# A spare buffer of 32 bytes in front of the row vector of the conditioning input

## The chip, the cores and the metric

The kernel runs on one core of one Trainium2 chip. The metric is the time of one execution on the device, in microseconds (us), lower is better. On the core five engines work side by side: TensorE (PE in the profile, its weight loads are listed apart as PEld), VectorE (DVE), ScalarE (ACT), GpSimd (POOL) and SyncE (SP), which issues most of the DMAs. Each has an instruction stream of its own, and semaphores order them. SBUF is the on-chip memory of 128 partitions, in which a buffer takes the same byte range in every partition. PSUM has eight banks that take TensorE's results.

## What is computed

Two transformer-like blocks, one after the other, on one sequence of 512 tokens of width 1024, all in float32. The first is a gated short convolution beside a stick-breaking attention, then an MLP, with scales and shifts made from a conditioning vector `c`. The second is a gated convolution of 31 taps beside a rotary attention with grouped keys, then attention to a memory of 256 rows, then a gated feed-forward layer with a convolution of 3 taps. Cut to what matters:

```python
def first_block(x, c, ...):
    mod = c @ w_ada[l] + b_ada[l]
    sh1, sc1, gt1, sh2, sc2, gt2 = jnp.split(mod, N_MOD, axis=-1)
    h = modulate(rms_norm(x, g_pre_mix[l]), sh1, sc1)
    proj = h @ w_in[l]
    ...
    x = x + gt1[:, None, :] * rms_norm(mix_out, g_post_mix[l])
    h2 = modulate(rms_norm(x, g_pre_mlp[l]), sh2, sc2)
    ff = jnp.square(jax.nn.relu(h2 @ w_mlp_in[l])) @ w_mlp_out[l]
    x = x + gt2[:, None, :] * rms_norm(ff, g_post_mlp[l])

def second_block(x, mem, ...):
    x = x + rmsnorm(parallel_mixer(rmsnorm(x, ...), ...), norm_mix_post[l])
    x = x + rmsnorm(memory_cross_attention(rmsnorm(x, ...), rmsnorm(mem, ...), ...), norm_mem_post[l])
    x = x + rmsnorm(conv_gated_ffn(rmsnorm(x, ...), ...), norm_ffn_post[l])
```

## The kernel before

Every large product runs on TensorE as three products of rounded parts. A weight slab of 1 MB (128 partitions by 2048 numbers) comes from HBM into one of the two halves of `w_raw`. GpSimd makes `w_hi` of it (the number rounded to the float32r format, line 602) and `w_lo` (the rest, line 604). ScalarE and VectorE make the same two parts of the other operand (`ht_hi` and `ht_lo`, `hq_hi` and `hq_lo`, `yt_hi` and `yt_lo`, `hf_hi` and `hf_lo`). `mm3`, lines 687 to 689, then issues hi by hi, lo by hi and hi by lo into one PSUM bank. In the profile the name in front of the comma is the moving operand, which streams past the array, and the one behind it is the stationary operand, which is loaded before each matmul: `bank<-ht_hi,w_hi` moves 512 tokens of `ht_hi` past 128 columns of `w_hi`, and `bank<-w_hi,hq_hi` moves 512 columns of `w_hi` past 128 tokens of `hq_hi`.

The stages follow one another: the first 33 us load `x` and the modulation weights (`ada_w`, seven buffers of 4 KB a partition) and sum them on VectorE (`ada_acc`, line 1662), then come the input product of the first block, its attention (about 209 to 340 us), the output product, the MLP (430 to 770 us), the second block's mixer with the convolution of 31 taps (`av`, shared by VectorE, GpSimd and TensorE, about 855 to 985 us), the attention to the memory, and the feed-forward layer (1200 to 1565 us).

All of SBUF is laid out by `sb(...)` calls, in program order, lines 265 to 375: a buffer starts where the last one ended, rounded up to a multiple of 32 bytes, and buffers in a closed `lend` or `ph` stack give their place to the next ones. Nothing else in the program depends on where a buffer lies. What matters below is the start of each buffer modulo 64 bytes, by the layout of the built program:

| Buffers | start modulo 64, before |
|---|---|
| `w_raw`, `w_hi`, `w_lo`, `x`, `ident`, `ones`, `vec` (all made ahead of `c_row`) | 0 |
| `c_row`, `gpost`, `stat`, `smx`, `qks`, `eps_t` | 0 |
| `xn`, `tmp`, `p2b`, `p2c`, `p2d`, `ht_hi`, `ht_lo`, `ada_w`, `ada_acc`, `mem`, `mem_k`, `mem_v`, `m1`, `at1`, `q1`, `k1`, `mg`, `yt_hi`, `yt_lo`, `sgb`, `hq_hi`, `hq_lo`, `hr`, `facc`, `qm`, `pm`, `ptm`, `av`, `uc`, `hf_hi`, `hf_lo`, `facc2` | 32 |
| `b1`, `ay`, `p2a`, `pt2`, `tap_m`, `rope`, `rope_m`, `qf` | 0 |

Of the kernel before, what the change touches and what calls it, by code (L numbers as in the profile page):

```python
# [25 lines left out]
P = 128  # L26
# [228 lines left out]
def build(nc, A, out):  # L255
    with ExitStack() as ctx:
        def sb(name, shape, dt=F32, where=None):
            return (where or ctx).enter_context(nc.sbuf_tensor(name, shape, dt))
# [15 lines left out]
        mod = sb("mod", [P, 4, DC])  # L274
        cvec = sb("cvec", [P, DC])
        mod_g = sb("mod_g", [P, DC])
        c_row = sb("c_row", [DC, P])
        gpost = sb("gpost", [P, 2, D])
        stat = sb("stat", [P, 64])
# [1899 lines left out]
```

How the kernel before makes its waits and increments, by code:

```python
    def after(self):  # L161
        if self.last is not None:
            self.eng.wait_ge(*self.last)
# [257 lines left out]
            def wait_free(self, eng):  # L422
                if not self.first:
                    eng.wait_ge(psum_free[self.b], self.use)
# [1 line left out]
            def wait_full(self, eng):  # L426
                eng.wait_ge(psum_full[self.b], self.use + 1)
# [1 line left out]
            def wait_taken(self, eng):  # L429
                eng.wait_ge(psum_free[self.b], self.use + 1)
# [22 lines left out]
        @block.sync  # L453
# [6 lines left out]
            def load(view, src, at=None):  # L460
                nonlocal n
                num = n if at is None else at
                if at is not None or n >= 2:
                    sp.wait_ge(slab_split, num - 1)
                sp.dma_start(view[n % 2], src).then_inc(slab_loaded[n % 2], 16)
                n += 1
# [7 lines left out]
            def ada(i):  # L475
                r = i % ADA_BUFS
                if i >= ADA_BUFS:
                    sp.wait_ge(ada_used, i - ADA_BUFS + 1)
                s = i // DC
                sp.dma_start(ada_w[:, r], wada[:, i % DC, s * D:(s + 1) * D]).then_inc(ada_loaded[r], 16)
# [5 lines left out]
            win = w_rows(A["w_in"])  # L486
            i = 2 * DC
            for c0 in (512, 1024, 0, 1536, 2048, 2560):
                for s in range(2):
                    if n == 1:
                        sp.wait_ge(ada_used, 2 * DC)
                    load(raw4, win[:, 4 * s:4 * s + 4, c0:c0 + 512])
                    for _ in range(4 if n > 2 else 0):
```

## Time and profile before

| | us |
|---|---|
| median of 3 runs | 1587.15 |
| lowest and highest of them | 1586.88, 1588.55 |
| the profiled execution's own time | 1588.48 |
| its span, from the first to the last instruction | 1586.6 |
| PE busy in the span | 1512.0 (95%) |
| POOL busy | 864.2 (54%) |
| DVE busy | 735.4 (46%) |
| ACT busy | 413.6 (26%) |
| mean granted clock of TensorE | 0.984 |

The table is read from the top: the execution's own time is 1.9 us over its span, and 1.33 us over the median of the three timed runs. TensorE is busy in 95% of the span, and the others in about half of it or less. A busy TensorE says nothing of how fast each matmul went by, since matmuls overlap; for that the distance from one start to the next is read from the timeline.

### The profile page before, as it was taken

The page shows a single profiled execution, that of the slowest core. Times are in us where ns is not written, and L with a number is a line of the kernel's source. Part 1 is how long each engine was busy: PE and PEld are TensorE (multiplying, and loading weights), DVE is VectorE, ACT ScalarE, POOL GpSimd, SP SyncE. Part 2 cuts the span into 40 slices and gives each one's busy share as a digit, 9 for nine tenths or more (in the row PEclk, how much of TensorE's full clock was granted, in tenths as well). Part 3 has the DMA queues.
Part 4 walks back from the last instruction along what each step waited for, and adds up shares of the span by engine and source line. Part 5 has one row for each costly group of instructions (what it writes and reads, how often), then busy time and mean ns, then how long its engine had stood idle before and what let it go on. Part 6 is the DMA issues. An engine that isn't in the chain of part 4 may idle for free.

```text
span 1586.6 us, 18794 instructions
## 1 busy us (share of the span) xinstructions
PE 1512.0 (95%) x7119; PEld 1197.7 (75%) x7119; DVE 735.4 (46%) x1067; ACT 413.6 (26%) x833; POOL 864.2 (54%) x333
## 2 busy tenths in 40 slices
PE   3999999999999999999899899999998999999997
PEld 3788767778988888888798644688687788888886
DVE  6795167752831111112333976341516544455445
ACT  3101133331520100101334166452414211111113
POOL 1666344345665655556567994175054656565652
PEclk8999999999999999999999999999999999999999
DMA  8874221223323232322243101032021332323231
GB/s 323 333 267 156 94 80 54 82 80 104 120 80 106 80 106 81 104 88 97 85 135 99 61 1 53 27 107 94 27 80 54 106 106 80 106 79 106 80 106 53
DMA packets 91765, 161.87 MB, mean 102 GB/s; under 512 B 3453, under 2 KB 44337, under 8 KB 91697
## 3 DMA queue, kind: packets, MB, share of 16 engines
q1 hardware_dynamic: 88720, 155.20, 28.8%
q10 hardware_dynamic: 2977, 5.73, 1.0%
q8 instruction: 47, 0.77, 0.2%
q14 instruction: 21, 0.17, 0.0%
HBM read 158.82 MB, written 2.10 MB: 101 GB/s over the span
## 4 chain that ended last, share of the span: by engine, by line
PE 78%; DVE 13%; ACT 4%; POOL 2%; issue 2%; DMA 1%; POOLq 0%; SPq 0%; DVEq 0%; ACTq 0%
PE bank L687 24%; PE bank L689 24%; PE bank L688 24%; DVE bank L1662 3%; DVE bank L1658 1%; POOL w_lo L604 1%; DVE smx L2024 1%; PE bank L1090 1%; DVE ada_acc L1662 1%; DVE x L1658 1%; DVE ht_lo L1658 1%; DMA ada_w<-in_w_ada 1%; DVE q L1658 1%; PE bank L1161 1%; PE bank L1142 1%
## 5 line engine op out<-in xcount | busy, mean ns | idle before, releaser
L602 POOL TENSOR_SCALAR w_hi<-w_raw 128x2048 fp32r<-128x2048 f32 x119 | 229.5, 1928 | 630.4 <-PE bank L687 602.5
L604 POOL TENSOR_TENSOR w_lo<-w_raw,w_hi 128x2048 fp32r<-128x2048 f32 x119 | 554.4, 4658 | 9.9
L687 PE MATMUL bank<-ht_hi,w_hi 128*128 128x512 f32 (+1 forms) x1200 | 448.5, 374 | 13.7 <-DVE ht_lo L1658 8.2
L688 PE MATMUL bank<-ht_hi,w_lo 128*128 128x512 f32 (+1 forms) x1200 | 445.3, 371 | 0.0
L689 PE MATMUL bank<-ht_lo,w_hi 128*128 128x512 f32 (+1 forms) x1200 | 445.3, 371 | 0.0
L687 PEld LDWEIGHTS bank<-ht_hi,w_hi 128*128 128x128 f32 x1200 | 226.1, 188 | 62.4 <-DVE ht_lo L1658 10.3
L689 PEld LDWEIGHTS bank<-ht_lo,w_hi 128*128 128x128 f32 x1200 | 226.0, 188 | 43.4
L688 PEld LDWEIGHTS bank<-ht_hi,w_lo 128*128 128x128 f32 x1200 | 226.1, 188 | 42.5
L1662 DVE SCALAR_TENSOR_TENSOR uc<-bank,par,uc 128x511 f32<-128x511 f32 x88 | 66.0, 750 | 162.9 <-ACT uc L1628 161.2
L1658 DVE TENSOR_TENSOR facc<-bank,facc 128x512 f32<-128x512 f32 x104 | 72.0, 692 | 123.5 <-PE bank L689 115.8
L1628 ACT ACTIVATE uc<-bank,par 128x512 f32<-128x512 f32 x44 | 34.3, 780 | 268.6 <-PE bank L689 257.3
L687 PE MATMUL bank<-w_hi,hq_hi 128*128 128x512 f32 x256 | 101.3, 396 | 0.0
L688 PE MATMUL bank<-w_hi,hq_lo 128*128 128x512 f32 x256 | 101.3, 396 | 0.0
L689 PE MATMUL bank<-w_lo,hq_hi 128*128 128x512 f32 x256 | 101.3, 396 | 0.0
L1447 ACT ACTIVATE hr<-bank 128x512 f32<-128x512 f32 x32 | 19.2, 600 | 271.3 <-PE bank L689 270.5
L687 PE MATMUL bank<-w_hi,ht_hi 128*128 128x512 f32 x224 | 89.5, 399 | 0.0
L689 PE MATMUL bank<-w_lo,ht_hi 128*128 128x512 f32 x224 | 88.6, 395 | 0.0
L688 PE MATMUL bank<-w_hi,ht_lo 128*128 128x512 f32 x224 | 88.6, 395 | 0.0
L1662 DVE SCALAR_TENSOR_TENSOR ada_acc<-ada_w,cvec,ada_acc 128x1024 f32<-128x1024 f32 x42 | 74.8, 1781 | 17.8 <-DMA ada_w<-in_w_ada 14.3
L1658 DVE TENSOR_TENSOR bank<-bank,hr 128x512 f32<-128x512 f32 x32 | 22.4, 699 | 128.0 <-ACT hr L1447 128.0
L689 PE MATMUL bank<-w_lo,hf_hi 128*128 128x512 f32 x176 | 70.1, 398 | 0.0
L687 PE MATMUL bank<-w_hi,hf_hi 128*128 128x512 f32 x176 | 69.3, 394 | 0.1
(258 smaller groups left out, 2054.7 us busy)
## 6 DMA issues: line engine op xcount, KB each, us to landing
w_raw<-in_w_in SPq DMA_DIRECT2D x27, 1024.0 KB, 5.2
ada_w<-in_w_ada SPq DMA_DIRECT2D x48, 512.0 KB, 7.5
w_raw<-in_w_up SPq DMA_DIRECT2D x22, 1024.0 KB, 5.1
w_raw<-in_w_mlp_in SPq DMA_DIRECT2D x16, 1024.0 KB, 5.2
w_raw<-in_w_mlp_out SPq DMA_DIRECT2D x16, 1024.0 KB, 5.1
w_raw<-in_w_down SPq DMA_DIRECT2D x11, 1024.0 KB, 4.9
w_raw<-in_w_out SPq DMA_DIRECT2D x8, 1024.0 KB, 5.0
w_raw<-in_w_mem_kv SPq DMA_DIRECT2D x8, 1024.0 KB, 5.5
```

The source lines that it names most:

```text
L602: g.tensor_scalar(w_hi[:, r], w_raw[:, r], 1.0, 1.0, ALU.mult, ALU.mult).then_inc(slab_hi, 1)
L604: g.tensor_tensor(w_lo[:, r], w_raw[:, r], w_hi[:, r].bitcast(F32), ALU.subtract).then_inc(slab_split, 1)
L687: inc_free(pe.matmul(o, ah, bh, start=start, stop=False))
L688: pe.matmul(o, al, bh, start=False, stop=False)
L689: return pe.matmul(o, ah, bl, start=False, stop=stop)
L1090: ins = pe.matmul(t.ap[HD * j:HD * j + HD, :], v2[:, kc, v], pt2[:, j, kc], start=kc == 0, stop=kc == NT - 1)
L1142: ins = pe.matmul(t.ap[:, 0:NM], qm[:, 2 * h + c, qt * P:qt * P + P], mem_k[:, 2 * h + c, :], start=c == 0, stop=c == 1)
L1161: ins = pe.matmul(t.ap[:], mem_v[:, kc, h * MHD + c * P:h * MHD + c * P + P], ptm[:, kc], start=kc == 0, stop=kc == MT - 1)
L1447: st.done(act.activation(hr[:, m % 2], t.ap[:], ACT.Relu), hr_ready)
L1628: st.done(act.activation(uc[:, c], t.ap[:], ACT.Identity, scale=par[:, p, 2 + g, k:k + 1], bias=par[:, p, 6 + g, k:k + 1]), uc_ready)
L1658: do(v.tensor_tensor(o, a, b, op), sem, tile)
L1662: do(v.scalar_tensor_tensor(out=o, in0=a, scalar=s, in1=b, op0=op0, op1=op1), sem, tile)
```

## The change

One buffer of 8 numbers a partition (32 bytes) is made ahead of `c_row`. No instruction reads or writes it. All buffers made behind it, `c_row` among them, lie 32 bytes higher; `w_raw`, `w_hi`, `w_lo`, `x`, `ident`, `ones`, `before`, `not_before`, `vec`, `mod`, `cvec` and `mod_g` stay. The highest buffer still ends inside SBUF. Every engine has the same instructions in the same order with the same semaphores, only the addresses of operands differ, and line numbers behind the new line are one higher.

```diff
--- before.py
+++ after.py
@@ -274,6 +274,7 @@
         mod = sb("mod", [P, 4, DC])
         cvec = sb("cvec", [P, DC])
         mod_g = sb("mod_g", [P, DC])
+        spare = sb("spare", [P, 8])
         c_row = sb("c_row", [DC, P])
         gpost = sb("gpost", [P, 2, D])
         stat = sb("stat", [P, 64])
```

In the table of the section on the kernel, the second row of buffers goes from 0 to 32 modulo 64, the third from 32 to 0, the fourth from 0 to 32; the first stays at 0. Modulo 256, `ada_w` goes from 160 to 192, `gpost` from 0 to 32, and `mem` and `ada_b` from 224 to 0; `w_raw` stays at 128.

## Rows read from the trace of the kernel before

**Rows 1.** Page, head, busy time (share of span) by engine, instructions
```profile
span 1586.6 us, 18794 instructions
...
PE 1512.0 (95%) x7119; PEld 1197.7 (75%) x7119; DVE 735.4 (46%) x1067; ACT 413.6 (26%) x833; POOL 864.2 (54%) x333
```

**Rows 2.** Page, chain of work that ended last, shares of the span by engine
```profile
PE 78%; DVE 13%; ACT 4%; POOL 2%; issue 2%; DMA 1%; POOLq 0%; SPq 0%; DVEq 0%; ACTq 0%
```

**Rows 3.** Waits, whole span: who waited for whom, us in total, times, longest
```profile
POOL w_hi L602 <- PE bank L687: 602.5, 102, 38.9
```

**Rows 4.** Timeline, PE, `ht` moving past `w`: start us, us, engine, line, instruction
```profile
59.73 0.39 PE L687 MATMUL bank<-ht_hi,w_hi 128*128 128x512 f32 x1
...
61.83 0.40 PE L687 MATMUL bank<-ht_hi,w_hi 128*128 128x512 f32 x1
```

**Rows 5.** Timeline, PE, `w` moving past `hq`
```profile
479.62 0.40 PE L689 MATMUL bank<-w_lo,hq_hi 128*128 128x512 f32 x1
...
481.72 0.40 PE L689 MATMUL bank<-w_lo,hq_hi 128*128 128x512 f32 x1
```

**Rows 6.** Timeline, PE, 256 columns, where the clock rises from 1.2 to 2.4 GHz
```profile
1201.08 0.41 PE L689 MATMUL bank<-ht_lo,w_hi 128*128 128x256 f32 x1
...
1203.63 0.41 PE L689 MATMUL bank<-ht_lo,w_hi 128*128 128x256 f32 x1
...
1204.75 0.28 PE L689 MATMUL bank<-ht_lo,w_hi 128*128 128x256 f32 x1
...
1205.93 0.28 PE L687 MATMUL bank<-ht_hi,w_hi 128*128 128x256 f32 x1
```

**Rows 7.** Groups of PE by form: count, busy us, mean ns, idle before
```profile
L687 PE MATMUL bank<-ht_hi,w_hi 128*128 128x512 f32 x944 | 375.1, 397 | 6.7 <-POOL w_lo L604 5.5 <-DVE ht_lo L1658 1.2
...
L687 PE MATMUL bank<-w_hi,hq_hi 128*128 128x512 f32 x256 | 101.3, 396 | 0.0
...
L687 PE MATMUL bank<-w_hi,ht_hi 128*128 128x512 f32 x224 | 89.5, 399 | 0.0
...
L687 PE MATMUL bank<-w_hi,hf_hi 128*128 128x512 f32 x176 | 69.3, 394 | 0.1
L687 PE MATMUL bank<-yt_hi,w_hi 128*128 128x512 f32 x64 | 26.4, 413 | 1.7 <-DVE yt_lo L1658 1.7
...
L1078 PE MATMUL bank<-ident,p2c 128*128 128x128 f32 x32 | 5.0, 278 | 0.0
L1078 PE MATMUL bank<-ident,p2a 128*128 128x128 f32 x32 | 4.9, 276 | 0.0
```

**Rows 8.** Instructions on `av`: ns min/median/max, first and last start
```profile
L1662 DVE SCALAR_TENSOR_TENSOR bank<-av,vec,bank x58: 754/756/758, 863.1 to 975.2; 128x512 f32<-128x512 f32 x58
...
L1103 PE MATMUL bank<-av,tap_m x52: 590/592/697, 925.4 to 984.0; 128*128 128x512 f32 x52
L639 POOL TENSOR_SCALAR tmp<-av,vec x30: 682/692/1130, 858.5 to 944.8; 128x512 f32<-128x512 f32 x30
```

**Rows 9.** Groups of DVE by form, sums and parts of 512 numbers
```profile
L1658 DVE TENSOR_TENSOR facc<-bank,facc 128x512 f32<-128x512 f32 x104 | 72.0, 692 | 123.5 <-PE bank L689 115.8 <-DVE x L1662 0.5
...
L1658 DVE TENSOR_TENSOR x<-bank,x 128x512 f32<-128x512 f32 x32 | 22.1, 692 | 1.1
```

**Rows 10.** Timeline, GpSimd and VectorE at the start of the first attention
```profile
212.26 4.62 POOL L604 TENSOR_TENSOR w_lo<-w_raw,w_hi 128x2048 fp32r<-128x2048 f32 x1
...
213.60 3.43 DVE L1658 TENSOR_TENSOR m<-m,not_before 128x128 f32<-128x128 f32 x1
```

**Rows 11.** Instructions on `m`: ns min/median/max, first and last start
```profile
L1658 DVE TENSOR_TENSOR m<-m,not_before x32: 292/295/3435, 211.2 to 322.9; 128x128 f32<-128x128 f32 x32
```

**Rows 12.** Busy time by stretch, us, then clock, DMA share, GB/s
```profile
20.00:27.00 7.00, 4.33 (x24) 4.24 (x24) 6.47 (x6) 0.70 (x1) 0.00 (x0) 0.99 1.03 411
...
36.00:38.00 2.00, 2.00 (x11) 1.98 (x11) 1.57 (x6) 1.48 (x3) 2.00 (x2) 0.50 1.05 404
```

**Rows 13.** Instructions on `gpost`, time of its five loads to landing
```profile
DMA to landing us min/median/max: 3.7/4.8/12.0
```

## The prediction, on record before the changed kernel ran

> **What bounds the kernel now.** I read the head of the page first: TensorE is busy for 1512.0 of 1586.6 us, the next engine, GpSimd, for 864.2 [rows 1], and the mean granted clock is 0.984 (table above). The chain of the work that ended last says the same: 78% of it is TensorE [rows 2], and GpSimd, which prepares the weights, waited for TensorE 102 times, 602.5 us in all [rows 3]. So nearly anywhere the time is the number of matmuls times the distance from one start to the next. The groups by form give the number: the hi by hi matmuls of 512 columns are 944 + 256 + 224 + 176 + 64 = 1664, and lines 688 and 689 have as many each, 4992 in all [rows 7]. The distance comes from the timeline, not from the durations in the groups, which overlap: nine starts take 61.83 - 59.73 = 2.10 us, 233.3 ns each [rows 4].
>
> That distance is not what the array itself would need, and this is what makes a change of addresses worth a look. Where the clock was still at 1.2 GHz, matmuls of 256 columns started 2.55 us / 12 = 212.5 ns apart; at 2.4 GHz ten of them took 1.18 us, 118 ns each [rows 6]. Half of 212.5 is 106, so at full clock some 12 ns for 256 columns, or by the same share 233.3 - 212.5 = 21 ns for 512 columns, come from something that does not speed up with the clock. If that something is the reading of SBUF, the start of an operand could bear on it.
>
> **The change, part by part.** It adds a buffer that nothing reads or writes, and no instruction, DMA or wait is added, removed or moved. What is left is the cost of an address that is 32 bytes higher, for each kind of reader and writer.
>
> Matmul, moving operand. Before, `ht` starts at 32 modulo 64 and `w` at 0. With `ht` moving the distance is 233.3 ns [rows 4]; with `w` moving nine starts take 481.72 - 479.62 = 2.10 us, 233.3 ns again [rows 5]. The two roles are exchanged between these stretches, so each of the two starts has been seen as the moving and as the stationary operand, at one price to within 0.01 us over nine matmuls, or 1.1 ns each. The mean durations of the five groups, 394 to 399 ns without the small one of `yt` (413), say the same [rows 7]. Moving `ht`, `yt` and stationary `hq`, `hf` from 32 to 0 is therefore 4992 x 0 = 0 us. The bound from the resolution is 4992 x 1.1 = 5.5 us either way; I take 0, because the same 233 ns recurs over the whole program.
>
> Matmul, plain float32. The convolution of 31 taps reads `av` from tap k on, that is from 31 starts 4 bytes apart, which pass both 0 and 32 modulo 64. Of 52 matmuls the median is 592 ns and the shortest 590; a few reach 697, too few to move the median, and a price of half the starts would move it [rows 8]. Transposes of `p2c` (32 modulo 64) and `p2a` (0) take 278 and 276 ns on average [rows 7]. Cost 0.
>
> VectorE and GpSimd. The same sliding reads take 754 to 758 ns on VectorE, all 58 of them, and a median of 692 ns on GpSimd [rows 8]. A sum into `x` (0 modulo 64) and one into `facc` (32) both take 692 ns [rows 9]. If the 4 ns of the first spread were all the address, some 1000 VectorE instructions would cost 4 us at most, of which 13% lie on the chain [rows 2]: 0.5 us. I take 0. GpSimd's two large steps work on `w_raw`, `w_hi` and `w_lo` alone, which do not move.
>
> DMA. `w_raw` stays, so only the opening, where VectorE waits for `ada_w`, could feel it. While the loads go to `ada_w` (32 modulo 64) the queues move 411 GB/s, and while they go to `w_raw` (0 modulo 64) 404 GB/s, both with the engines fully busy [rows 12]. If `ada_w` at 0 took the other rate, the 33 us ahead of the first product would change by 33 x 7 / 411 = 0.6 us; I take 0 and keep 0.6 both ways. `gpost` goes from 0 to 32; its loads take 3.7 to 12.0 us to land [rows 13], two of them under the first product and one in each later stage, long before their use, and would have to become several times longer to be seen.
>
> The sum is 0 against the profiled execution's own 1588.48 us, which lies 1.33 us above the median of the three runs. Against the median the forecast is 1587.15, say 1587.2 us.
>
> [...]
>
> **The rivals.** (a) *A pair of starts that has not been seen, and is cheaper.* In every float32r matmul before, one operand is at 0 and the other at 32 modulo 64; after, both are at 0. The exchange of roles above excludes a price of either alone, not of the pair. If the 21 ns over the half-clock distance are a collision between the read of the moving operand and the load of the next stationary one, and equal starts end it, the kernel gains up to 4992 x 21 = 105 us and lands at about 1482. For it speaks only that the 21 ns are unexplained. Against it: the surplus grows with the moving columns (12 ns at 256, 21 at 512) while the stationary load is the same 128 columns [rows 4, 6], so it does not look like a collision with the load. 4%.
>
> [...]
>
> (b) *The same pair, and dearer; slower.* Place: the same 4992 matmuls. If equal starts make the two reads meet where they now pass each other, by as much as the surplus that is already there, the cost is the same 105 us with the other sign, 1692 us. It decides early: 3.2 us / 4992 = 0.64 ns a matmul is already 0.2% of the time. The transposes are a small counter-example: `p2a` and `ident` both start at 0 and are no slower than `p2c` with `ident` [rows 7], but they read at half the rate. 3%.
>
> (c) *Other meetings of GpSimd and VectorE.* At 213.60 us a VectorE multiply took 3.43 us and ended 0.15 us after GpSimd's 4.62 us subtraction [rows 10], where the median of its kind is 0.295 us [rows 11]: it waited for it, by 3.1 us, in the attention stage, where VectorE is on the chain. A shift of a few tenths of a microsecond could add or take away such a meeting. But the streams have no new length that would shift them, and the three runs of before, in which DMA timing differs anyway, agree within 1.7 us. One meeting gives 1584 or 1590; to pass 0.2% it takes more than one. 3% on each side.
>
> (d) *The change does nothing because the layout hides it*, for instance if buffers were rounded to 64 bytes. They are rounded to 32, so all later buffers do move; if not, the time would be 1587 too.
>
> **How the numbers follow.** No effect: 87%, 1587.2, with its own spread from the runs of before (1586.9 to 1588.6), the 0.6 us of the opening and one meeting of (c), 3.1 us, each way: 1584.0 to 1590.3. That range leaves out (a), (b) and the far part of (c), less than 2 in 10, so it stands as the range. About 0.2% (3.2 us) is what a measurement of this kernel can tell from no change. Faster by more: 4% of (a) and 3% of (c), 7%. Slower by more: 3% of (b) and 3% of (c), 6%. Within 0.2%: the rest, 87%.
>
> **What would show it right or wrong.** In the changed kernel's profile the starts of nine matmuls near 60 and near 480 us should again take 2.10 us; the groups of `ht`, `hq` and `hf` should keep 394 to 399 ns; VectorE's taps 756 ns, sums into `facc` 692 ns; the stretch of 20 to 27 us about 411 GB/s. If the nine starts take less than 2.09 or more than 2.11 us, (a) or (b) is true and the step "each start has been seen, so the pair is free" has failed. If the distances are the same and the time is not, the difference must stand in the waits: in the durations of `m` on VectorE between 209 and 325 us (c), or in the start of the first product at 39 us (DMA).

## The result, and the profile after

The changed kernel took 1578.17 us, the median of six runs from 1573.54 to 1583.45, against 1588.27 us for the kernel before in its six runs (1586.88 to 1588.55). The ratio is 0.9938, with a 95% interval of 0.9915 to 0.9961: it is 0.6% faster, by 10.1 us, and its runs differ by 9.9 us where those of before differ by 1.7. The forecast of no change was wrong, and the time lies below the range of 1584.0 to 1590.3.

The page of the changed kernel, head, busy time by engine and the chain's shares (beside [rows 1, 2]):

```profile
span 1575.5 us, 18794 instructions
...
PE 1500.7 (95%) x7119; PEld 1200.9 (76%) x7119; DVE 731.9 (46%) x1067; ACT 413.4 (26%) x833; POOL 868.7 (55%) x333
...
PE 82%; DVE 10%; ACT 3%; POOL 2%; issue 1%; DMA 1%; POOLq 0%; SPq 0%; DVEq 0%; ACTq 0%
```

TensorE's busy time fell by 11.3 us with the same 7119 matmuls, and the span by 11.1. The busy times of the other engines moved by at most 4.5 us. The place is found on the timeline of PE, in three kinds of stretch; each pair of lines is nine matmul starts apart. `ht` moving past `w`, as in [rows 4]:

```profile
59.99 0.39 PE L688 MATMUL bank<-ht_hi,w_hi 128*128 128x512 f32 x1
...
62.05 0.39 PE L688 MATMUL bank<-ht_hi,w_hi 128*128 128x512 f32 x1
```

`w` moving past `hq`, as in [rows 5]:

```profile
480.03 0.39 PE L690 MATMUL bank<-w_lo,hq_hi 128*128 128x512 f32 x1
...
482.13 0.40 PE L690 MATMUL bank<-w_lo,hq_hi 128*128 128x512 f32 x1
```

`w` moving past `hf`, in the last stage, after the change and then before it:

```profile
1252.11 0.39 PE L690 MATMUL bank<-w_lo,hf_hi 128*128 128x512 f32 x1
...
1254.17 0.39 PE L690 MATMUL bank<-w_lo,hf_hi 128*128 128x512 f32 x1
```

```profile
1255.07 0.40 PE L689 MATMUL bank<-w_lo,hf_hi 128*128 128x512 f32 x1
...
1257.17 0.40 PE L689 MATMUL bank<-w_lo,hf_hi 128*128 128x512 f32 x1
```

With `ht` moving the nine starts take 2.06 us, 228.9 ns each, where they took 2.10 us. With `w` moving past `hq` they still take 2.10 us. With `w` moving past `hf` they take 2.06 where they took 2.10. So three stretches that looked alike before (233.3 ns all) now part. The mean durations of the groups by form hide most of this; the lines beside [rows 7]:

```profile
L688 PE MATMUL bank<-ht_hi,w_hi 128*128 128x512 f32 x944 | 372.0, 394 | 6.1 <-POOL w_lo L605 5.3 <-DVE ht_lo L1659 0.8
...
L688 PE MATMUL bank<-w_hi,hq_hi 128*128 128x512 f32 x256 | 101.3, 396 | 0.0
```

The mean of the `ht` group went from 397 to 394 ns while the distance went down by 4.3. The other readers of shifted buffers are where they were. Instructions on `av` and on `m` (beside [rows 8, 11]):

```profile
L1663 DVE SCALAR_TENSOR_TENSOR bank<-av,vec,bank x58: 754/756/756, 857.2 to 970.4; 128x512 f32<-128x512 f32 x58
...
L1104 PE MATMUL bank<-av,tap_m x52: 590/592/697, 920.6 to 979.2; 128*128 128x512 f32 x52
L640 POOL TENSOR_SCALAR tmp<-av,vec x30: 688/692/1147, 852.5 to 938.3; 128x512 f32<-128x512 f32 x30
```

```profile
L1659 DVE TENSOR_TENSOR m<-m,not_before x32: 292/294/3447, 209.7 to 320.3; 128x128 f32<-128x128 f32 x32
```

Sums into `facc` still take 692 ns, and the loads of the opening (the stretch of 20 to 27 us, all into `ada_w`, as in [rows 12]) moved 408 GB/s for 411.

**Where the 11.1 us of span come from.** Over all steps in the two traces, 2832 matmuls with `ht` moving came 4.3 ns closer each (233.3 to 229.0), which is 12.2 us; 528 with `w` moving past `hf` came 4.2 ns closer, which is 2.2 us. The matmuls of 256 columns, whose distances I worked out from the starts in the two traces, went two ways: 960 with `ht` or `mt` moving from 116.8 to 117.8 ns (1.0 us lost), 192 with `w` moving past `mt` from 118.2 to 113.5 (0.9 us gained). Together 14.3 us. Some 3 us were given back, most of them in two places: the first product began at 39.5 us for 39.0, and in the second attention the granted clock stayed at 0.50 for longer. Busy time by stretch, before and then after; the column behind those of the engines is the granted clock:

```profile
905.00:916.00 11.00, 5.50 (x26) 3.77 (x26) 7.53 (x7) 2.66 (x4) 10.09 (x11) 0.77 0.00 0
```

```profile
905.00:916.00 11.00, 8.48 (x15) 3.50 (x16) 3.02 (x5) 2.58 (x5) 10.09 (x11) 0.53 0.00 0
```

The mean granted clock of these 11 us is 0.77 before and 0.53 after; ahead of the fall TensorE had waits between short pieces of work in both kernels (busy for 2.59 us of 905 to 911 before and for 0.83 us of 900 to 905 after). The low stretch went from 911.0 to 917.8 us before (6.8 us) and from 905.6 to 915.9 us after (10.2 us). The part of the stage that took 105.1 us before (901.7 to 1006.7) took 106.7 us after (895.1 to 1001.9).

### The profile page after: what moved, and what is told of

Same layout as the page of the kernel before. It is cut to its first block, busy times and chain, and to the rows that moved or that the text cites. A ratio compares the mean times of both kernels' runs of the same rounds, so it can differ in the third digit from the quotient of the medians.

```text
span 1575.5 us, 18794 instructions
## 1 busy us (share of the span) xinstructions
PE 1500.7 (95%) x7119; PEld 1200.9 (76%) x7119; DVE 731.9 (46%) x1067; ACT 413.4 (26%) x833; POOL 868.7 (55%) x333
## 4 chain that ended last, share of the span: by engine, by line
PE 82%; DVE 10%; ACT 3%; POOL 2%; issue 1%; DMA 1%; POOLq 0%; SPq 0%; DVEq 0%; ACTq 0%
PE bank L688 25%; PE bank L690 25%; PE bank L689 25%; DVE bank L1663 2%; DVE bank L1659 1%; POOL w_lo L605 1%; DVE smx L2025 1%; PE bank L1091 1%; DVE ada_acc L1663 1%; DVE x L1659 1%; DMA ada_w<-in_w_ada 1%; DVE ht_lo L1659 1%; PE bank L1162 1%; PE bank L1143 1%; DVE m L1659 1%
## 5 line engine op out<-in xcount | busy, mean ns | idle before, releaser
L603 POOL TENSOR_SCALAR w_hi<-w_raw 128x2048 fp32r<-128x2048 f32 x119 | 232.8, 1956 | 612.6 <-PE bank L688 585.5
L688 PEld LDWEIGHTS bank<-ht_hi,w_hi 128*128 128x128 f32 x1200 | 226.4, 189 | 56.6 <-DVE ht_lo L1659 10.1
L689 PEld LDWEIGHTS bank<-ht_hi,w_lo 128*128 128x128 f32 x1200 | 226.4, 189 | 39.5 <-issue 0.2
L689 PE MATMUL bank<-w_hi,hf_lo 128*128 128x512 f32 x176 | 69.3, 394 | 0.0
```

The lines of the kernel that those rows point to most:

```text
L603: g.tensor_scalar(w_hi[:, r], w_raw[:, r], 1.0, 1.0, ALU.mult, ALU.mult).then_inc(slab_hi, 1)
L688: inc_free(pe.matmul(o, ah, bh, start=start, stop=False))
L689: pe.matmul(o, al, bh, start=False, stop=False)
```

## The experiments

### The changed kernel once more

The kernel is the changed one, unedited.

> The changed kernel once more, for a second profile and for the spread of its times, which went from 1573.5 to 1583.5 us in six runs where the kernel before stayed within 1.7 us. If the distance between matmul starts is fixed by addresses alone, this profile shows the same distances as the first one of the changed kernel (228.9 ns with ht moving, 229.1 with w moving past hf, 233.3 with w moving past hq or ht), and the spread comes from elsewhere. If the distance depends on a phase that differs between executions, some of these groups differ from the first profile by 1 ns or more, and explain a difference in time of 3 us or more.

1577.78 us (1574.88 to 1578.68, four runs), ratio 0.994, interval 0.9923 to 0.9957: the gain is there again. The distances with 512 columns were 228.96 ns with `ht` moving and 233.32 with `w` moving past `hq`, to 0.01 ns as in the first profile. The 256-column matmuls were not: of the first two groups with `mt` moving, 117.8 and 117.8 ns in the first profile, one had 113.3; the last long group with `ht` moving had 113.3 for 117.8. `yt` in its first product had 232.4 for 233.6. These account for about 1 of the 2.6 us by which the two spans (1575.5 and 1572.9) differ. The other 1.6 us arose between 178 and 186 us, where the granted clock was 0.50 for 6.8 us in the first profile and for 3.4 us in the second. Busy time by stretch, in the first profile and then in the second:

```profile
178.00:189.00 11.00, 11.00 (x39) 7.96 (x39) 5.51 (x12) 0.59 (x1) 3.99 (x2) 0.69 0.13 50
```

```profile
178.00:189.00 11.00, 11.00 (x46) 7.89 (x46) 5.29 (x12) 0.74 (x2) 5.25 (x2) 0.84 0.13 50
```

In the same 11 us TensorE got 39 matmuls in at a mean granted clock of 0.69, and 46 at 0.84. So the starts of the buffers fix most distances, at some of them more than one pattern is possible (117.8 or 113.3 ns), and the length of the low stretches of the clock (6.8 or 3.4 us) moves the time as well.

### 64 bytes instead of 32, and everything 32 bytes higher

```diff
-        spare = sb("spare", [P, 8])
+        spare = sb("spare", [P, 16])
         c_row = sb("c_row", [DC, P])
```

> The spare buffer is 64 bytes instead of 32: ht, hq, hf and the others lie 64 bytes higher than before and start at 32 modulo 64 again. Theory A (the start modulo 64 bytes decides): 233.3 ns everywhere, about 1588 us. Theory B (any change of the distance between the two operands decides, with a period over 64 bytes): distances other than 233.3 ns in at least one group, and a time that differs from 1588 by more than 3 us.

```diff
+        spare = sb("spare", [P, 8])
         w_raw = sb("w_raw", [P, 2, SLAB])
...
-        spare = sb("spare", [P, 8])
         c_row = sb("c_row", [DC, P])
```

> The spare buffer of 32 bytes stands in front of w_raw instead of c_row, so that every buffer lies 32 bytes higher, w_hi and w_lo too: ht is where it is in the changed kernel, and its distance to w is that of before. Theory C (the place of the two operands relative to each other decides): 233.3 ns everywhere, about 1588 us. Theory D (the start of ht, hf alone decides): 228.9 ns with ht moving, about 1578 us, as the changed kernel.

Both diffs are against the changed kernel. With 64 bytes the time was 1592.2 us, ratio to the kernel before 1.0022 (1.0013 to 1.0032): a little slower. With all buffers 32 bytes higher it was 1588.8, ratio 1.0008 (0.9998 to 1.0017): the same. Timeline of PE with all buffers higher, `ht` moving:

```profile
60.02 0.39 PE L688 MATMUL bank<-ht_hi,w_hi 128*128 128x512 f32 x1
...
62.12 0.40 PE L688 MATMUL bank<-ht_hi,w_hi 128*128 128x512 f32 x1
```

2.10 us for nine starts, as before, though `ht` lies exactly where it lies in the changed kernel, at 0 modulo 64. Theory D (the start of `ht` alone) is out, and theory C (the two operands' places relative to each other) stands. With the spare of 64 bytes, `w` moving past `hq`:

```profile
479.97 0.40 PE L689 MATMUL bank<-w_hi,hq_lo 128*128 128x512 f32 x1
...
482.08 0.39 PE L689 MATMUL bank<-w_hi,hq_lo 128*128 128x512 f32 x1
```

2.11 us, and over all matmuls of this kind in the trace 234.3 ns for 233.3, while `ht` moving stayed at 233.4. Every shifted buffer is where it was before modulo 64, and a group still changed: the period is longer than 64 bytes, so theory A is out too. Most of the 4.4 us that this kernel lost (1592.2 for 1587.8) lies in the matmuls of 256 columns, though: 960 with `ht` or `mt` moving went from 116.8 to 119.9 ns, 3.0 us, and 1440 of 512 columns with `hq` or `ht` stationary went up by 1.0 ns, 1.4 us.

### The table of pairs

A kernel that runs nothing but groups of 32 matmuls from one moving and one stationary start:

```python
for m, s, n in [GROUPS[0]] + GROUPS:
    a, b = (m - MOV) // 4, (s - STA) // 4
    for k in range(N):
        ins = pe.matmul(bank0[:, 0:n], sta[:, b:b + P], mov[:, a:a + n], start=k == 0, stop=k == N - 1)
```

> This kernel leaves the whole computation out (it copies x to the output) and runs only groups of 32 float32r matmuls, all other engines idle: 64 groups with the moving start at 0 to 224 and the stationary start at 0 to 224 bytes beyond a common base in steps of 32, then finer steps of 4 bytes, then 128, 256 and 384 columns. If the pair of starts decides (theories A and C), the groups differ by 4 ns or more a matmul along one or both of the starts. If the difference comes from other engines' reads and writes at other addresses (theory E), every group of 512 columns has one distance, to within 1 ns.

The distance in ns, worked out from the starts in its trace (the first four steps of a group left out). Both buffers begin at the same place modulo 256:

```
stationary   moving +0     32     64     96    128    160    192    224
+0               227.0  233.3  228.9  233.3  233.5  234.3  233.4  233.2
+32              233.1  226.7  233.3  228.9  233.3  232.5  234.3  233.3
+64              233.4  233.1  226.8  233.3  228.9  233.3  233.2  234.4
+96              234.4  233.3  233.1  227.1  233.3  228.9  233.3  232.1
+128             232.4  234.2  233.4  233.4  227.1  233.3  228.9  233.3
+160             233.7  232.1  234.1  233.4  233.4  227.5  233.3  228.9
+192             228.9  233.7  232.4  234.3  233.4  233.2  226.7  233.3
+224             233.3  229.0  233.3  232.5  234.3  233.4  233.4  227.6
```

The table is nearly constant along its diagonals, those that wrap around included: in steps of 32 bytes the difference, moving start minus stationary start, modulo 256 bytes fixes the distance to within 1 ns. Only +128 spreads more, from 232.1 to 233.5. 0 gives 227, +64 gives 228.9, the others 232 to 234.4. The other engines are idle here, so theory E (their traffic) is out. The trace itself shows it for the first three groups; the timeline merges equal instructions, and (duration - 0.39) / (count - 1) is the distance: 227, 234 and 229 ns.

```profile
15.93 2.89 PE L77 MATMUL bank<-mov,sta 128*128 128x512 f32 x12
```

```profile
23.57 2.73 PE L77 MATMUL bank<-mov,sta 128*128 128x512 f32 x11
```

```profile
31.13 2.68 PE L77 MATMUL bank<-mov,sta 128*128 128x512 f32 x11
```

Now nearly every group of the full kernels falls into place. `w_hi` and `w_lo` start at 128 modulo 256; the differences and what the two tables (this one, and the one of 256 columns below) and the traces say:

```
                          before             changed            64 bytes
ht moving, 512            +32  233.3         +64  229.0         +96  233.4
w moving past hq, 512     -32  233.3         -64  233.3         -96  234.3
w moving past hf, 512     +96  233.4         +64  229.1         +32  233.3
mt moving, 256            +32  117.0         +64  117.8/115.8   +96  119.8
w moving past mt, 256     -32  118.3         -64  113.5         -96  118.4
table at +32 233.3, +64 228.9, +96 233.3, -32 233.2, -64 233.4, -96 234.3
```

The change had put the matmuls with `ht` moving, and those with `w` moving past `hf`, at a difference of +64, the best place in steps of 32 bytes besides 0; those with `hq` stationary went to -64, which is no better than -32. `yt`, not in this list, went from +96 to +128: 233.4 ns before, 233.6 and 232.3 after in its two products, within what the table shows at +128. With 256 columns two places don't fit the table below: `mt` moving at +64 mostly has 117.8 ns where the table has 113.3, and `w` moving past `mt` at -96 has 118.4 where it has 117.4.

### Once more, and in steps of 4 bytes

> The kernel of pairs once more. If the distances are fixed by the starts, every group is as in pairs to within 0.5 ns. If a group can fall into more than one pattern, as the 256-column groups at difference +64 did in the two profiles of the changed kernel (117.8 and 113.3 ns), some groups differ by 2 ns or more.

All 64 groups are as in the first profile, to 0.1 ns. In this setting there is one pattern a pair.

Behind the 64 groups the kernel of pairs has some more. In seven of them the stationary start goes up by 4 bytes a group, to +28, and the moving one stays. The kernel below, `fine`, in which the moving start goes in steps of 4 bytes, is to be read beside them.

```diff
-                        ins = pe.matmul(bank0[:, 0:n], sta[:, b:b + P], mov[:, a:a + n], start=k == 0, stop=k == N - 1)
+                        ins = pe.matmul(bank0[0:cols, 0:n], sta[:, b:b + cols], mov[:, a:a + n], start=k == 0, stop=k == N - 1)
```

> Leaves the whole computation out, as the kernel of pairs did, and runs 64 groups of 32 matmuls in which the moving start goes in steps of 4 bytes over 256 bytes, then 256 and 128 columns at steps of 32 bytes, then starts that are 256 to 16384 bytes further, then 64 and 32 stationary columns instead of 128. Theory F (only the difference of the starts modulo 256 bytes counts): the starts 256 to 16384 bytes further give the 226.7 to 227.0 ns of difference 0. Theory G (the surplus over 213.3 ns comes from the load of the next stationary operand, as it reads SBUF beside the moving one): with 64 stationary columns the surplus falls to about half, with 32 to about a quarter, at each difference. Theory H (the surplus belongs to the moving columns alone): it stays at 13 to 20 ns with 64 and 32 stationary columns.

The period of theory F holds: with the moving start 256, 512, 1024, 2048, 4096, 8192 or 16384 bytes further, 226.9 to 227.0 ns. In steps of 4 bytes the distance runs between 226.7 and 240.0 ns with no simple order (ns; the stationary start stays, and the number ahead of each row is how many bytes further the moving one starts):

```
  0   227.0 236.5 233.5 228.9 231.5 240.0 233.3 226.7
 32   233.3 234.8 233.3 229.9 233.4 233.3 230.1 226.7
 64   228.9 236.6 235.6 228.3 231.1 234.2 233.3 231.6
 96   233.3 240.0 230.0 226.7 231.1 240.0 240.0 230.1
128   232.4 236.2 233.3 231.1 233.3 233.3 234.8 226.7
160   234.3 237.4 233.3 230.1 233.3 238.0 233.3 230.1
192   233.2 233.9 233.3 231.1 234.6 238.8 234.3 230.0
224   233.3 240.0 233.3 228.9 236.8 240.0 230.0 226.7
```

Nothing falls below 226.7. But at steps finer than 32 bytes theory F's other half fails: the difference alone doesn't fix the distance. With the stationary start 4, 8, ... 28 bytes further and the moving one at its base, the kernel of pairs gave 232.4, 230.4, 233.3, 226.7, 233.3, 230.0 and 233.3 ns, and its second run the same to 0.1 ns. The table has the same differences modulo 256 at moving starts of 252, 248, ... 228 bytes: 226.7, 230.0, 240.0, 236.8, 228.9, 233.3 and 240.0 ns. The widest gap is at a difference of -16, first by the stationary start (+16), then by the moving one (+240):

```profile
649.32 2.43 PE L77 MATMUL bank<-mov,sta 128*128 128x512 f32 x10
```

```profile
481.17 2.53 PE L76 MATMUL bank<-mov,sta 128*128 128x512 f32 x10
```

That is 227 and 238 ns by these ten, and 226.7 and 236.8 over the groups. So the rule of the difference is shown for starts at multiples of 32 bytes, which all buffers of the full kernels have.

With 256 columns and differences of 0, 32, ... 224 bytes it is 119.8, 116.8, 113.3, 120.1, 120.0, 117.4, 113.3, 118.3 ns: 0 is bad there, and +64 and -64 are best. With 128 columns it is 111.7 at all eight, and with 384 columns 173.7 and 173.3 ns at 0 and 32 bytes. Theory G fails: with 64 stationary columns 230.0, 230.8 and 228.4 ns at 0, 32 and 64 bytes, with 32 columns 231.5, 233.2 and 231.1. The surplus doesn't shrink with the load; only the spread between the starts does, from 6.3 ns to 2.4 and 2.1. Theory H had the size right: 15 to 20 ns over 213.3 are left with 64 and 32 columns. The 213.3 is an estimate for 512 columns at the full clock, half of the 426.7 ns that they took at a granted clock of 0.50 (six starts in 2.56 us, 135.14 to 137.70 us, in the second profile of same256). But the surplus doesn't belong to the moving columns alone, since the stationary operand's place counts.

### The rule used on the full kernel

```diff
+        spare = sb("spare", [P, 56])
         c_row = sb("c_row", [DC, P])
```

> The spare buffer is 224 bytes. Modulo 256 bytes the difference of moving and stationary start becomes 0 for ht and hq in both roles, 128 for w moving past hf and 64 for yt moving. If the table measured in pairs holds in the full kernel: 226.7 to 227 ns with ht moving and with w moving past hq and ht, 233.4 ns with w moving past hf, 228.9 ns with yt moving. Matmuls of 512 columns: 2832 with ht moving, 768 and 672 with w moving past hq and ht, 6.5 ns less each than before, 27.8 us; yt 192 x 4.4 = 0.8 us; 1588 - 28.6 = 1559, give or take 4 us for the narrower ones. If the full kernel with its traffic follows another rule, at least one of these distances is off by over 1 ns.

```diff
+        spare = sb("spare", [P, 56])
         c_row = sb("c_row", [DC, P])
...
+        spare_y = sb("spare_y", [P, 48], where=ph)
         yt_hi = sb("yt_hi", [P, CC, T], F32R, where=ph)
...
+        spare_f = sb("spare_f", [P, 32], where=ph)
         hf_hi = sb("hf_hi", [P, 2, 2, T], F32R, where=ph)
```

> As spare224, and two more spare buffers, 192 bytes in front of yt_hi and 128 bytes in front of hf_hi, so that the two operands of every float32r matmul start at the same place modulo 256 bytes. By the table of pairs all 4992 matmuls of 512 columns come 6.5 ns closer, 32.4 us against before, and 528 x 6.5 - 0.8 + 192 x 6.5 - 0 = 4 us against spare224: 1555 us. If what was gained comes back as waits for GpSimd or VectorE, the distances are 226.7 ns and the time is above 1560.

Both diffs are against the kernel before. spare224 took 1562.99 us (ratio 0.9849, 0.9824 to 0.9874), with 226.8 ns for `ht` moving, 226.7 past `hq`, 232.4 past `hf` (forecast 233.4) and 229.0 for `yt`. same256 took 1559.72 us (0.9831, 0.9811 to 0.985), with 226.7 to 226.9 ns for all 512-column matmuls. Its timeline, `ht` moving:

```profile
59.90 0.39 PE L690 MATMUL bank<-ht_hi,w_hi 128*128 128x512 f32 x1
...
61.94 0.39 PE L690 MATMUL bank<-ht_hi,w_hi 128*128 128x512 f32 x1
```

2.04 us for nine. The distances are as forecast, and the times are 4 to 5 us above the forecasts: 3.2 us are the 1152 matmuls of 256 columns, which I had left at their old price and which now take 119.8 ns instead of 116.8 to 118.3, as the table of 256 columns has it. Another 1.1 us is the starting point: the forecasts reckon from 1588, and the kernel before took 1589.1 beside these two.

### 256 columns at 64 bytes, and what the spread is

```diff
+        spare_m = sb("spare_m", [P, 16])
         mt_hi = sb("mt_hi", [P, DC, NM], F32R)
...
+        spare_q = sb("spare_q", [P, 48], where=ph)
         hq_hi = sb("hq_hi", [P, DC, T], F32R, where=ph)
...
-        spare_f = sb("spare_f", [P, 32], where=ph)
+        spare_f = sb("spare_f", [P, 16], where=ph)
```

> As same256, but mt, whose matmuls are all 256 columns wide, starts 64 bytes off w modulo 256. By the table of fine, 192 matmuls with mt moving and 192 with mt stationary go from 119.8 to 113.3 ns, 384 x 6.5 = 2.5 us: 1557 us beside the 1560 of same256. If the two patterns at difference 64 come up here too, those with mt moving may stay at 117.8, and the gain is 1.6 us.

> same256 once more, beside best on the same chip, and for a second profile of it: 1560 us, distances within 0.3 ns of the first profile. If the spread of its runs (1558.2 to 1564.5) comes from patterns that differ between executions, a group differs by over 1 ns; if all groups agree, the spread comes from elsewhere (the granted clock's windows).

The diff is against same256. On one chip, five runs each: 1559.27 us (0.9823, 0.9807 to 0.9839) and 1563.0 us (0.9832, 0.9814 to 0.985). The intervals overlap, so which of the two is faster isn't shown. In the profile the groups with `mt` in either role went from 119.7 to 117.8 ns, and one of those with `w` moving past `mt` to 113.8: some 0.8 us, not 2.5, since they mostly took the dearer of the two patterns.

The second profile of same256 has a span of 1561.9 us against 1556.2 in the first, with equal distances (to 0.1 ns in nearly all groups), so its spread isn't made of patterns. The largest piece is one wait of TensorE:

```profile
129.14 0.39 PE L692 MATMUL bank<-ht_lo,w_hi 128*128 128x512 f32 x1
133.97 0.47 PE L690 MATMUL bank<-ht_hi,w_hi 128*128 128x512 f32 x1 [4.44 <-DVE yt_lo L1661]
```

The first profile has no gap there. With the low clock that followed the wait (0.51 from 134.7 to 138.2 us), the second profile had lost 6.3 us against the first by 139 us, on top of 0.8 us from the opening; 3.3 us of that came back by 190 us, since the first profile has its low stretch at 176.9 to 183.7 us, and 1.5 us were lost again around 240 us, where only the second has one. What came ahead of it on VectorE, in the first profile and then in the second:

```profile
103.81 15.24 DVE L1665 SCALAR_TENSOR_TENSOR ada_acc<-ada_w,cvec,ada_acc 128x1024 f32<-128x1024 f32 x7
...
122.38 3.08 DVE L1661 TENSOR_TENSOR yt_lo<-bank,yt_hi 128x512 fp32r<-128x512 f32 x4
```

```profile
108.98 20.83 DVE L1665 SCALAR_TENSOR_TENSOR ada_acc<-ada_w,cvec,ada_acc 128x1024 f32<-128x1024 f32 x7
...
133.13 3.08 DVE L1661 TENSOR_TENSOR yt_lo<-bank,yt_hi 128x512 fp32r<-128x512 f32 x4
```

The same seven sums of the modulation weights took 15.24 us in one execution and 20.83 in the other. Most sums take 1.28 us. In the first profile one of the seven took 2.75 us and one 5.45, in the second two took 2.73 and two 5.44, and each of the long ones ended about 1.1 us after a long step of GpSimd (`w_hi` or `w_lo`) that it had met. One more such meeting, at 89.8 us, had already made the second profile begin the seven 5.2 us later. So `yt_lo`, which frees the PSUM banks, came 10.8 us later, and TensorE waited for them. That is rival (c) of the prediction, in the first product instead of the attention. The faster TensorE makes the wait longer but is not all of it: this matmul was due at about 129.4 us, in the kernel before it starts at 131.1, and the banks came free at 133.8, so by an estimate from these numbers the same delay would have cost the kernel before some 2.7 us. Whether such waits also make up the 9.9 us between the runs of the changed kernel is not shown: neither of its two profiles has that wait.

### Other types, and the patterns

> Leaves the whole computation out, as in pairs. First bfloat16 and plain float32 operands of 512 columns at differences 0 to 224 bytes. If the collision belongs to the rate at which the moving operand is read (float32r at 4 bytes a column is the fastest reader), bfloat16 and float32 show one distance to within 1 ns at all differences, near 213.3 and 429 ns; if every kind of read collides, they spread as float32r does. Then twelve groups of 256 float32r columns at difference +64, each behind a separator of another length: if this difference has two patterns that the start of a group picks, both 113.3 and 117.8 ns come up; if not, all show 113.3. Then 64 rows instead of 128: the same distances as with 128 rows if the reads decide. Last, groups of three as the kernel has them, the low parts at differences of their own: each matmul shows the distance of its own pair if only the pair counts.

The kernel is that of pairs with operands of three types, `types` by its label. bfloat16 keeps 215.8 ns and plain float32 429.2 ns at all eight differences, to 0.05 ns (a float32 matmul leaves two records, each 429.2 ns behind the one before). Two of the bfloat16 groups, at differences of 0 and 128 bytes, on the timeline:

```profile
29.74 2.54 PE L84 MATMUL bank<-mov_b,sta_b 128*128 128x512 bf16 x11
```

```profile
53.65 2.55 PE L84 MATMUL bank<-mov_b,sta_b 128*128 128x512 bf16 x11
```

So of the three types only float32r is touched at these steps; it moves 4 bytes a column in about the time (226.7 to 234.4 ns) in which bfloat16 moves 2 (215.8 ns). That this rate is the reason is not shown, and steps finer than 32 bytes weren't run with the other two. The groups with 64 rows instead of 128 gave 226.8, 233.3 and 228.9 ns at 0, 32 and 64 bytes, as with 128 rows. The twelve groups of 256 columns at +64 all had 117.8 ns, whatever the separator, while the same difference had given 113.3 in `fine`: both patterns exist, but what picks one stays open. In groups of three with the stationary low part 32 bytes off, the mean was 233.3 ns (228, 233 and 239 in turn), not the 229 that the three pairs would average. With the moving low part 32 bytes off it was 231.4 ns (the pairs: 229), with both 232.2 (231), with both 64 bytes off 231.3 (230), and with all at one start 226.8. So in a mixed triple a matmul doesn't keep the distance of its own pair, and each of the four came out dearer than its pairs.

## Why the prediction was wrong, point by point

- **What bounds the kernel** was right: 4992 matmuls of 512 columns times a distance. So was the remark that an address could bear on the 21 ns that the half clock leaves unexplained. The runs put the part that good starts give back at 6.6 ns of it; no pair came below 226.7. What the rest is stays open. The two clocks that the prediction and [rows 6] give as 1.2 and 2.4 GHz the profile shows as shares alone, 0.50 from 1201.0 to 1203.6 us and 1.00 from 1204.7 to 1206.0 us; no run shows the figures in GHz.
- **Moving operand, 0 us.** This step failed. It took the exchange of roles between [rows 4] and [rows 5] as proof that starts cost nothing, and it asked for the start modulo 64 only. The difference was +32 in the one and -32 in the other modulo 256, and `hf` at +96: three places of the table that cost 233.1 to 233.7 ns. Equal prices at three places of a function of the pair say nothing of a fourth. Measured in its place: -4.3 ns a matmul in 3360 of the 4992, 14.4 us, where the sum had 4992 x 0. The matmuls of 256 columns, which the sum didn't have as a term, came to 0.1 us net.
- **Rival (a), the pair.** The right place, the pair of starts, with 4% and at 105 us. Its rule was not: it had both starts at 0 modulo 64 as the cheaper case, and `w` moving past `hq`, which is at 0 and 0 after the change, stayed at 233.3 ns. That the two reads collide is not shown either. Its counter-argument, that a surplus which follows the moving columns can't come from the meeting with the load, was what kept the chance low. The surplus hardly depends on the size of the load (64 or 32 stationary columns) and yet depends on its place: in the table of pairs the stationary start changes the distance by up to 7.6 ns at steps of 32 bytes (226.7 to 234.3 with the moving start at +192). So the argument was no argument. What the float32r reads share, if anything, no run shows. Its price took all 21 ns in all 4992 matmuls; it was 4.3 ns in two thirds.
- **Rival (b), dearer.** The same function on its other side. A spare of 64 bytes has it: 1.0 ns more past `hq` and 3.1 ns more with `ht` moving at 256 columns, 1592.2 us. The half rate of plain float32, which it named for the transposes, is there in the kernel of types: 429.2 ns a record (two to a matmul) where float32r has 226.8.
- **Plain float32, VectorE, GpSimd, DMA at 0** were right: 592, 754 to 756 and 692 ns, and 408 GB/s against 411. With `ada_w` at 224 modulo 256 (the spare of 64 bytes) the queues moved 411 GB/s too.
- **Rival (c)** didn't make the gain. It appeared where it had not been placed, as a wait of 4.4 us in one profile of same256.
- **The range** was made from the spread of the runs before and from rival (c), as if the unseen pair had no smaller prices than 105 us. The bound of 5.5 us from the timeline's resolution and the 0.6 us of the opening were also left out of it: 1584.0 to 1590.3 is 3.1 us each way. Nor was the spread of the kernel before as small as three runs made it look: in 19 later runs it took from 1585.9 to 1591.4 us.

## What to carry to other kernels

With float32r operands, lay both at the same start modulo 256 bytes for matmuls of 512 columns: 226.7 to 227.6 ns from start to start here, where +32 had 233.3. For 256 columns no place was safe: 64 bytes apart gave 113.3 ns or 117.8, and +32 gave 116.8 to 117.2. Look at the distance from start to start, not at mean durations, to see whether it worked; three spare buffers of 224, 192 and 128 bytes were worth 1.7% here. When a change alters addresses, list the pairs that each instruction reads together, with their difference at a period longer than you think needed (64 bytes was too short here, 256 held); prices seen at some differences don't bound the others. And a faster main engine can make a wait for the others longer: one was 4.4 us here and, by the estimate above, would have been some 2.7 in the kernel before.

## What the runs showed of the hardware that I had not expected

- Back-to-back float32r matmuls of 512 columns start 226.7 to 240.0 ns apart at a granted clock of 1.00, by the two operands' starts. At starts that are multiples of 32 bytes their difference modulo 256 bytes decides, to about 1 ns; at steps of 4 bytes it also matters which of the two starts is moved (226.7 or 236.8 ns at a difference of -16). bfloat16 had 215.8 and float32 429.2 ns at all eight differences tried, in steps of 32 bytes.
- The best difference depends on the width: 0 with 512 columns (226.7 to 227.6), +64 and -64 with 256 (113.3, but 117.8 in other executions), none with 128 (111.7 at all eight).
- At +64 bytes and 256 columns the same program had 117.8 ns in one execution and 113.3 in the next, over whole groups.
- What in the chip makes the difference count is open. The runs show that it doesn't need the other engines' traffic (226.7 to 234.4 ns in the table of pairs, with the others idle), that 64 rows do as 128 (226.8, 233.3 and 228.9 ns at 0, 32 and 64 bytes), and that the surplus doesn't shrink in proportion to the stationary columns (at the same three places 230.0, 230.8 and 228.4 ns with 64, 231.5, 233.2 and 231.1 with 32).
